# Routing tiles of 128, 128 and 32 tokens in a decoder trunk, with the sample rows held four times, and eight expert slots beside the ring

## What is computed

```python
h = rms_norm(x, g_ffn_l) * (1.0 + sc2) + sh2      # sh2, sc2: one row for the prompt, one for each sequence
p_grp  = softmax(h @ w_rg + b_rg)                 # 4 groups, best one taken
in_grp = (h @ w_re + b_re)[best group]            # 8 experts of that group
top_l, top_i = top_k(in_grp, 2)                   # two experts a token
combine = p_g * softmax(top_l)
# each of the 32 experts: (silu(xb @ w_eg[e]) * (xb @ w_eu[e])) @ w_ed[e], then summed with combine
```

## Time and profile before

| | us |
|---|---|
| median of 3 runs (1116.57 to 1120.71) | 1119.69 |
| profiled execution, its own time | 1124.9 |
| its span, first to last instruction | 1123.2 |
| PE busy / DVE / ACT / POOL | 984.6 / 382.0 / 299.2 / 72.8 |
| mean granted TensorE clock (share of full) | 0.953 |
| DMA mean rate | 284 GB/s |

### The profile page before, as it was taken

The page is one execution under the profiler, slowest core; times in us unless marked ns, Lnnn a source line. Parts: engine busy times, 40 slices in busy tenths (PEclk is TensorE's granted clock), DMA queues, the critical chain, the costliest instruction groups (busy, mean ns, idle before and its releaser), DMA issues.

```text
span 1123.2 us, 21790 instructions
## 1 busy us (share of the span) xinstructions
PE 984.6 (88%) x7612; PEld 630.6 (56%) x7613; DVE 382.0 (34%) x1079; ACT 299.2 (27%) x685; POOL 72.8 (6%) x149
## 2 busy tenths in 40 slices
PE   4899999899999997788979999999997999778795
PEld 2567677377855443344456767745785644334343
DVE  1127632223261332222342583131326133222234
ACT  2335554400133111011143455441003311011112
POOL 1112000000100000000001200000010000000000
PEclk9889998989998999998989999898998999999998
DMA  9993233995376999999994332289731399999981
GB/s 383 311 420 125 103 113 89 390 420 218 117 326 244 422 422 422 422 421 397 420 356 148 131 113 94 71 322 421 300 145 40 118 411 422 422 422 422 410 371 43
DMA packets 65429, 319.16 MB, mean 284 GB/s; under 512 B 6050, under 2 KB 27874, under 8 KB 28226
## 3 DMA queue, kind: packets, MB, share of 16 engines
q1 hardware_dynamic: 63408, 315.06, 70.2%
q10 hardware_dynamic: 1810, 2.51, 0.6%
q0 software_dynamic: 128, 0.40, 0.1%
HBM read 315.44 MB, written 2.51 MB: 283 GB/s over the span
## 4 chain that ended last, share of the span: by engine, by line
PE 67%; DMA 15%; DVE 8%; ACT 5%; issue 4%; SPq 1%; ACTq 0%; POOL 0%; DVEq 0%; PEldq 0%; POOLq 0%
PE ps L579 20%; DMA ring<-wstream 15%; PE ps L1020 8%; PE ps L656 7%; PE ps L951 4%; PE ps L997 4%; PE ps L1029 4%; PE ps L1010 4%; PE ps L612 3%; PE ps L1000 2%; PE ps L830 2%; PE ps L722 2%; DVE work L1374 1%; ACT work L1202 1%; DVE top L1373 1%
## 5 line engine op out<-in xcount | busy, mean ns | idle before, releaser
L1020 PE MATMUL ps<-ring,work 128*32 128x512 f32 x912 | 115.0, 620 | 30.8 <-DMA ring<-wstream 30.5
L579 PE MATMUL ps<-work,ring 128*128 128x288 f32 x512 | 132.6, 418 | 2.9 <-DVE work L1464 2.9
L579 PE MATMUL ps<-h,ring 128*128 128x288 f32 x512 | 134.4, 417 | 0.7 <-ACT work L1132 0.7
L579 PEld LDWEIGHTS ps<-work,ring 128*128 128x128 f32 x512 | 98.4, 195 | 30.5 <-issue 3.7
L656 PE MATMUL ps<-h,ring 128*128 128x288 f32 x416 | 107.5, 420 | 9.0 <-ACT h L1146 6.6
L579 PEld LDWEIGHTS ps<-h,ring 128*128 128x128 f32 x512 | 97.1, 194 | 29.7 <-issue 4.1
L1263 ACT ACTIVATE mraw<-ps 128x512 f32<-128x512 f32 x64 | 38.2, 598 | 251.3 <-PE ps L1020 249.2
L656 PEld LDWEIGHTS ps<-h,ring 128*128 128x128 f32 x416 | 81.0, 196 | 33.8 <-issue 11.2
L1613 DVE SCALAR_TENSOR_TENSOR h<-work 128x288 f32<-128x288 f32 x128 | 60.6, 515 | 108.7 <-issue 108.7
L1029 PEld LDWEIGHTS ps<-fold,mraw 128*128 128x128 f32 x512 | 64.0, 196 | 57.6 <-ACT mraw L1263 50.3
L1029 PE MATMUL ps<-fold,mraw 128*128 128x32 f32 x512 | 70.8, 283 | 27.0 <-PE ps L1010 18.6
(11 more groups left out here) (240 smaller groups left out, 989.0 us busy)
## 6 DMA issues: line engine op xcount, KB each, us to landing
ring<-wstream SPq DMA_DIRECT2D x274, 1024.0 KB, 15.4
work<-wstream SPq DMA_DIRECT2D x14, 1024.0 KB, 16.8
work<-pages SPq DMA_DIRECT2D x32, 192.0 KB, 3.4
work<-pages SPq DMA_DIRECT2D x32, 128.0 KB, 2.1
cs<-consts SPq DMA_DIRECT2D x1, 1218.0 KB, 8.9
x<-x_in SPq DMA_DIRECT2D x1, 1152.0 KB, 5.7
out_y<-h ACTq DMA_DIRECT2D x2, 576.0 KB, 2.8
out_vp<-work ACTq DMA_DIRECT2D x2, 256.0 KB, 3.0
```

The costliest lines, as they stand in the source:

```text
L579: last = mm(out, w[:, (k0 + k) * stride:(k0 + k) * stride + 128], rhs(k), start=(k == 0), stop=(k == n - 1))
L1020: last = mm(pgu[32 * c:32 * c + 32, :], xs[:, k, :], ws[k // 4][:, c * 512:(c + 1) * 512], start=(k < 4), stop=(k >= 4), skip_group_check= ...
```

## The change

- Tokens are tiled 128, 128 and 32 (third tile: the sample tokens alone). The third tile is held four times, one copy in each group of 32 rows, so that all operations still run on 128 rows.
- DVE writes the sample part of h four times (`hs4`). The shift of the sample tokens relative to the prompt's is turned on PE as a matrix of its own (`hs`, 16 matmuls into column groups), ACT copies the shift part, and DVE makes `hrow_s` with one operation. The jobs `h4`, `h5`, the spread of the factor (L915), its copy (L1233), POOL's two operations (L516, L518), and DVE's L1520 and L1522 go away. POOL makes the shift earlier, beside the `out` projections.
- The gather takes two matmuls of 128 rows for each block and half. For the third tile four blocks k share: `hrow_s` has block k in row group k mod 4, so four matmuls of 32 rows, one in each row group, end four blocks in four banks. The first four blocks use `pgu`, `pgut`, `py`, `pzs`, the others banks 0 to 3.
- `rows` and DVE's L1591 go away. Each `bc` job becomes three matmuls with a broadcast column as weights.
- Squares, counts and ranks get matmuls for the third tile.
- Eight extra slots (pairs 63 to 70) in place of seven: five issued at the projections, one at the `out` projections, two after the last gather. The constants lose 256 of their 2436 columns.

```diff
-EXTRA = 7
+EXTRA = 8
...
-                    for j in range(4):
+                    for j in range(5):
                         load_extra(of, j)
+                if i - RING in first_out:
+                    load_extra(first_out[i - RING], 5)
...
-                    for j in range(4, EXTRA):
+                    for j in range(6, EXTRA):
...
-                step(sample_norm, nc.gpsimd.tensor_tensor(h[:, :, NP:T], h[:, :, NP:T], bc(rms[:, NP:T].unsqueeze(1), [128, KD, NS]), ALU.mult))
-                hs = by_seq(h[:, :, NP:T], KD)
-                step(sample_norm, nc.gpsimd.tensor_tensor(hs, hs, bc(shift_s.unsqueeze(3), [128, KD, NB, TS]), ALU.add))
...
+                ps = job("hs")
+                sample_shift.wait(pe, l)
+                for k in range(KD):
+                    c, at = k % 4, k // 4 * 128
+                    mm(ps[32 * c:32 * c + 32, at:at + 128], hs4[:, k, 0:NS], ident, start=True, stop=True)
+                for k in range(KD):
+                    c, at = k % 4, 256 + k // 4 * 128
+                    last = mm(ps[32 * c:32 * c + 32, at:at + 128], shift_s[:, k, :], ident,
+                              start=True, stop=True)
+                filled(last, "hs")
...
-                counted.up(mm(pgut[:, 96:192], cs[0:TB, C_ONE:C_ONE + 128], hot[0:TB, :, :], start=True, stop=True))
+                mm(pgut[:, 96:160], ones, hot[:, 0:2, :], start=True, stop=True)
+                counted.up(mm(pgut[:, 160:192], ones[0:NS, :], hot[0:NS, 2, :], start=True, stop=True))
...
-                    for tb in range(3):
-                        last = mm(ps[:, 0:T], hrow[0:TB, tb, k * 128:(k + 1) * 128], sel[0:TB, tb, hf * T:(hf + 1) * T],
-                                  start=(tb == 0), stop=(tb == 2))
...
+                            for tb in range(2):
+                                mm(outs[-1][:, 0:T], hrow[:, tb, k * 128:(k + 1) * 128], sel[:, tb, part],
+                                   start=(tb == 0), stop=False, skip_group_check=True)
+                        for c in range(4):
+                            last = mm(outs[c][:, 0:T], hrow_s[32 * c:32 * c + 32, k0 // 4 * 128:k0 // 4 * 128 + 128],
+                                      sel[32 * c:32 * c + 32, 2, part], start=False, stop=True, skip_group_check=True)
...
-                    filled(mm(ps[:, 0:T], cs[0:4, C_ONE:C_ONE + 128], rows4[0:4, i, :], start=True, stop=True), f"bc{i}")
+                    for tb in range(3):
+                        n = (128, 128, NS)[tb]
+                        last = mm(ps[:, tb * 128:tb * 128 + n], bc(dest[0:n, 7 + i, tb:tb + 1], [n, 128]), ident[0:n, 0:n],
+                                  start=True, stop=True)
+                    filled(last, f"bc{i}")
...
+                banks.done(V.scalar_tensor_tensor(hrow_s, ps[:, 0:256], dest[:, 15, 2:3], yb[:, :], ALU.mult, ALU.add), l, "hs")
                 counted.wait(d, l)
...
-                for i in range(4):
-                    ins = V.tensor_scalar(rows4[0:4, i, :], banks.ap(l, "rows")[0:4, 0:T], ident[0:4, i:i + 1], None, ALU.mult)
```

More of the change, by code:

```diff
@@ L51 @@
 SB = [(i * 128, min(128, SLOTS - i * 128)) for i in range((SLOTS + 127) // 128)]
-C_ID, C_ROT, C_ONE, C_LOW, C_SUM, C_ROW = (i * 128 for i in range(6))
-C_HEAD = 896
+C_ID, C_ONE, C_LOW, C_SUM, C_ROW = (i * 128 for i in range(5))
+C_ROT = C_ONE
+C_HEAD = 640
 C_COS = C_HEAD + 4
 C_SIN = C_COS + T
-C_CB0 = C_SIN + T
-C_CB1 = C_CB0 + 128
+C_CB1 = C_SIN + T
+C_CB0 = C_CB1 + 128
 C_SM = C_CB1 + 256
@@ L87 @@
 GATHERS = [(k, hf) for hf in range(2) for k in range(KD)]
[L88 to L90 removed]
+FAR = 4
 NEXT_EARLY = 2
@@ L113, in plan @@
     jobs += [f"out{m}" for m in range(KD)]
-    jobs += [f"h{n}" for n in TURNS] + ["rank"]
-    for i, (k, hf) in enumerate(GATHERS):
-        if i == ROWS_AT:
-            jobs += ["rows"]
-        if i == NEXT_AT and l + 1 < DEPTH:
+    jobs += [f"h{n}" for n in range(4)] + ["hs", "rank"]
+    for hf in range(2):
+        jobs += [f"x{k}.{hf}" for k in range(FAR, KD)]
+        if hf == 0 and l + 1 < DEPTH:
             jobs += ["next_t"]
-        jobs += [f"x{k}.{hf}"]
     jobs += [f"bc{i}" for i in range(4)]
@@ L290, in decoder_trunk @@
         squared = carve(0, KD, T)
-        drow = carve(4864, 4, T)
-        slot = carve(4864 + 4 * T, N_EXP * MAXBLK)
-        shift_s = carve(8352, KD, NB)
-        rt = [carve(4864 + i * 128, 128) for i in range(10)]
-        hrow = carve(6304, 3, D)
-        xs = carve(6304, KD, BLK)
-        sg = carve(6560, 2, BLK)
-        hdn = carve(6624, 2, BLK)
+        lg = carve(3648, 3, 36)
+        d4, g4 = carve(3756, 3, N_GRP), carve(3768, 3, N_GRP)
+        le, d32, hot1, hot2, tmp32, hot = (carve(at, 3, N_EXP) for at in (3780, 3876, 3972, 4068, 4256, 4352))
+        e4 = wi[:, :, :]
+        slot = rms[:, :]
+        shift_s = carve(8192, KD, NS)
+        hs4 = carve(7168, KD, 128)
+        hrow = carve(4864, 2, D)
+        hrow_s = carve(6912, 256)
+        sel = carve(7168, 3, SLOTS)
+        sg, hdn = cnt[:, 0:2, :], cnt[:, 2:4, :]
         gu = mraw[:, :]
-        zs_rows = carve(4864, 256)
-        sel = carve(9376, 3, SLOTS)
-        extra = [carve(6688 + i * PAIR, PAIR) for i in (3, 4, 5, 6, 0, 1, 2)]
-        per_row = wrow[0:TB, 5:8]
+        zs_rows = carve(2304, 256)
+        extra = [carve(4864 + i * PAIR, PAIR) for i in (3, 4, 5, 6, 7, 2, 0, 1)]
         hflat = h[:, :, :].rearrange("p k t -> p (k t)")
-        rows4 = hflat[:, 0:4 * T].rearrange("p (i t) -> p i t", t=T)
+        drow = hflat[:, 0:4 * T].rearrange("p (i t) -> p i t", t=T)
+        xs = hflat[:, 7 * T:7 * T + KD * BLK].rearrange("p (k s) -> p k s", s=BLK)
         hit = [hflat[:, (4 + i) * T:(5 + i) * T] for i in range(2)]
@@ L424, in _ @@
             first_projection = {AT[l, P_PROJ]: l for l in range(DEPTH)}
+            first_out = {AT[l, P_OUT]: l for l in range(DEPTH)}
             pages1_at = {RING: 0, AT[1, P_QI] + RING: 1}
@@ L891, in _, with square_sums @@
                 sq_added.wait(pe, l)
-                for tb in range(3):
-                    mm(pgut[0:TB, tb:tb + 1], sq_sum[:, tb * TB:(tb + 1) * TB], ones[:, 0:1], start=(tb == 0), stop=False,
-                       skip_group_check=True)
+                def square_sums(of, first):
+                    for tb in range(2):
+                        mm(pgut[:, tb:tb + 1], of[:, tb * 128:(tb + 1) * 128], ones[:, 0:1], start=(first and tb == 0), stop=not first,
+                           skip_group_check=True)
+                    for c in range(4):
+                        last = mm(pgut[32 * c:32 * c + 32, 2:3], of[:, NP:T], ones[:, 0:1], start=False, stop=not first,
+                                  skip_group_check=True)
+                    return last
+                square_sums(sq_sum, True)
                 sq.wait(pe, l, KD)
-                for tb in range(3):
-                    last = mm(pgut[0:TB, tb:tb + 1], sqt[1][:, tb * TB:(tb + 1) * TB], ones[:, 0:1], start=False, stop=True,
-                              skip_group_check=True)
+                last = square_sums(sqt[1], False)
                 ss.up(last)
@@ L902, in _ @@
                 assert not used_up, used_up
-                def turn_h(n):
+                for n in range(4):
                     ps = job(f"h{n}")
@@ L958, in _ @@
                         banks.wait_drained(pe, l, f"x{KD - 1}.0")
+                        far_kept.wait(pe, l)
                     c = k % 4
```

201 lines of the change are left out of this document (97 added, 104 removed).

## The result

The changed kernel takes 1128.4 us in the median of 11 runs, the kernel before 1119.7 us in 11 runs beside them: ratio 1.007, 95% interval 1.005 to 1.010. It is slower by 0.7%, where 1% faster was forecast. The profiled execution took 1131.32 us (span 1129.4; 1124.9 and 1123.2 before).

The account below looks back on a forecast made before the run. PE and the weight stream bound the kernel, with `x7.1` (routing chain plus gather) dating each layer's expert part. Layer 0 -5.7, layer 1 -5.5, start -0.3: -11.5 us off the median gives 1108.2, range 1102 to 1115.5.

Parts of the forecast that it names:

- The four expert stretches: Ring resumption to expert 20 and expert 20 to 31, both layers: lengths unchanged, 128.4 us kept, tail within 3 us.
- The rest: Everything outside the expert stretches: -5.7 us in layer 0, -5.5 in layer 1, -0.3 at the start.
- a gather at the lower clock: Rival: gather at half clock, over 0.5% slower; 1127 with one gather, 1145 with both; chance 0.06.
- the stalls: PE's waits on "issue" as written-out code moves: each 2 to 4 us either way; chance 0.04, 0.02 of it slower.
- The gather: Gather in each layer: 32 of 96 records replaced by four row-group sets, 5.6 us less.
- The set: Four row-group matmuls in the gather, eight records: 0.70 us a set, bounds 0.54 and 2.0.
- The job `rows`: PE job dropped with the gather change: counted as 0.4 us less in each layer.
- Start of the gather: Routing chain ahead of the gather: start 0.6 us earlier in layer 0, 0.4 in layer 1.
- the rank's five groups: Rank and counts on PE before the gather: two more small matmuls, 0.4 us in layer 0, 0.6 in layer 1.
- `bc`: Four jobs between the gather and the ring's resumption: 2.20 us become 2.64, 0.5 us added in each layer.
- Extra slots: Eighth slot and two late transfers for three: ring's resumption unmoved, more slack in the tail, 0 us gained.
- Constants: Load at the start, ahead of the first ring pieces: 256 of 2436 columns less, 0.3 us gained.

Follow-up runs that it names:

- the second profile: The changed kernel profiled again with nothing altered; ratio to the kernel before 1.007 (1.004 to 1.010).
- the two best kernels: Changed tiling, experts 24 to 31 looped, more parts altered: 0.985; the same with 28 wide unread products in layer 1 exchanged for 74 narrow: 0.982.

## Why the prediction was wrong

The profiled execution was forecast to change by -11.5 us and changed by +6.4. The four expert stretches, which the sum held constant, took 7.9 us more (5.6 by the second profile). The rest, for which -11.5 was added up, changed by -1.6 us (-4.9 by the second). Both steps failed, and by the first profile either alone puts the time above the range. The sign, slower, was in the prediction with a chance of 0.08, of which 0.06 was for another reason (a gather at the lower clock) and 0.02 for the stalls.

1. *The stretches held constant.* The prediction had itself "wrong" if the interval from ring to expert 20 did not keep its 128.4 us, or the tail changed by more than 3. The stalls on "issue" had been seen (2.1 us) and were given a chance of 0.04. By the profiles the experts took 3.0 us more in layer 0 (+3.7, -0.7) and 4.9 in layer 1 (+1.8, +3.0); by the second profile 1.3 (+2.6, -1.3) and 4.3 (-0.1, +4.4). The shift by 128 instructions, which took the ratio from 1.007 to 0.996, shows that such a difference is a matter of place: with its code elsewhere the changed kernel is not slower.
2. *The gather*: forecast 5.6 us less in each layer, measured 4.7 and 3.7. The set was right, 0.70. Records of 128 rows take 0.253 us (4.05 for 16) against 0.245 of 96 rows: 0.5 us. The job `rows` had cost 0.25 from its start to the next record (327.35 to 327.60), not its length of 0.41. In layer 1 the first 16 records go at half clock: 3.0 us lost, where 2.0 were lost before.
3. *Start of the gather*: `R_HOT` came 1.0 us earlier, as forecast. But the rank's five groups take 1.93 us (312.33 to 314.26) where I added 0.4 to 0.84. So PE and DVE met no sooner: 15.65 us became 15.7, or 17.4 where the clock falls in PE's new pause of 1.5 us; layer 1 14.8 became 15.6. Forecast: 0.6 and 0.4 less.
4. *`bc`*: forecast +0.5, measured 1.6 (L983, 0.165 a record). L915's 0.11 was for 96 columns of weights and 96 wide; these have 128, and the price was left as it was.
5. *Logits*: not priced. Each `out` block has L871 as four and two records with other weights, and its period went from 4.42 to 4.55 us: 1.0 us in a layer.
6. *Extra slots*: 0, as forecast. *Constants*: 384 columns go, not 256 (`C_CB0` lies within `C_CB1` as well), which by the prediction's rate is 0.5 us in place of 0.3. No profile shows even that: they landed at 11.36 us, and at 10.59 in the kernel before.

Points 2 to 6 make 1 to 3 us less in place of 11.5, so even with the experts untouched the forecast would have missed its range. The table, with the repeats, agrees: the rest is 718.8 us in the mean of nine profiles of the changed tiling (712.7 to 724.2) and 720.3 in five of the kernel before (717.1 to 723.1). What the measured times leave to the change, with the code of both lying nearly alike, is 0.1 to 0.3% (0.990 and 0.988 against 0.991), not told from nothing.

Open: why the band lies some 45 instructions lower in layer 1 and differs between the kernels (my count of what a product becomes may be off); why the same code at the same place loses 3 us more in one execution than in another (layer 0 of the two best kernels); why the clock falls in the same pause in some executions only; and the stretch from expert 31 to layer 1's last gain, 295.0 us in the changed kernel for 292.8, of which the logits explain 1.0. The profiles spread there over 288 to 296 us with the changed tiling and 287 to 293 without, so one pair of them can't settle it.

## What to carry to other kernels

Where code in a row is run while the DMA engines are full, look for idle time of PE put down to "issue" with a slow clock behind it, and compare it expert by expert: a change elsewhere can move it, and its sign is then not that of the change. See whether each such pause ends a short time behind a transfer of instructions. Insert a hundred instructions that do nothing and time again before believing a difference under 1%; keep code that is jumped over out of the stream of the hot part, or loop over a body that the engine holds, and look where the slow stretch has gone. And a pause of PE costs more than its length where long work follows it.

## What the runs showed of the hardware

- Instructions come in transfers of 16.4 KB, about 260 instructions, over DMA. 94 pauses of PE in 19 profiles end 1.2 to 2.4 us behind the end of one. A body of four experts (some 1,120 instructions) stays held: 2 transfers in 110 us of its later rounds, 11 in 70 us of code in a row.
- One pause of 1.5 us for code costs about 3 us, as the next expert runs at 1.2 GHz: 3.35 for 1.92 us. A band of slow experts in the tail costs 3 to 12 us (65.9 to 75.0 us against 63.1), and 1 to 5 where the ring's loading is the bound behind it (experts 1 to 4: 129.5 to 133.5 us against 128.4).
- The Trainium skill's "TensorEngine Tiling (Array Packing)", Key Properties, says that a change of tiling mode drains the engine. A set between 128-row work took 0.70 us, against 0.54 in a row of its like the earlier trace rows, or 0.61 by width (an estimate, 288 columns for 256): the drain is small, at most some 0.1 us a set.
